# h begins 16 bytes inside a larger tile, 80 bytes in front of the weights modulo 512 in place of 64

## The reference, cut to what matters

```
first block, twice (layer l):
  x += 0.5 * swiglu(rms_norm(x, ffn1_norm), w_gate, w_up, w_down)      # 1024 -> 2816 -> 1024
  h  = rms_norm(x, mix_norm);  a, g, q, k, v = split(h @ w_in)
  x += concat(conv_module(a, g), diff_attention(q, k, v)) @ w_out
  x += 0.5 * swiglu(rms_norm(x, ffn2_norm), ...)
second block, layer 0 and layer 1:
  h  = rmsnorm(x, norm_mix) * (1 + scale) + shift                      # scale, shift, gate from c
  x += gate * (retention_mixer(h) if layer 0 else sgu_mixer(h))
  h  = rmsnorm(x, norm_ffn) * (1 + scale) + shift
  x += gate * peer_ffn(h)          # 16384 experts: queries, top 16 of each of 8 heads, then
                                   # sum over the chosen experts of gelu(h . u_e) * g_e * v_e
x = rmsnorm(x, norm_final)
```

## The kernel before, in words

| tile | address before | modulo 512 |
|---|---|---|
| h_hi, h_lo | 12416, 20608 | 128, 128 |
| w_hi, w_lo | 64192, 80576 | 192, 192 |
| arena | 97408 | 128 |
| p_hi, p_lo (in the arena, float 29456 on) | 215232 on | 192 |

## Time and profile before

### The profile page before, as it was taken

One profiled execution on the slowest core, in us unless ns is written; L12 is line 12 of the kernel. 1 busy time (PEld: TensorE's weight loads), 2 busy tenths in 40 slices (PEclk: granted clock), 3 DMA queues, 4 the chain that ended last, 5 costly groups with the idle time before them and its releaser, 6 DMA issues.

```text
span 3093.0 us, 53282 instructions
## 1 busy us (share of the span) xinstructions
PE 3027.7 (98%) x22540; PEld 2855.6 (92%) x22540; DVE 2184.9 (71%) x3454; ACT 1605.3 (52%) x2383; POOL 274.3 (9%) x255
## 2 busy tenths in 40 slices
PE   8999999999999999999999999999999999999998
PEld 8998999999999898999999998878989998999887
DVE  5877887876887656799555557765659985555676
ACT  5565554565554454456544445547444554444444
POOL 0010001010101001830000000000157000000000
PEclk9999999999999999999999999999999999999999
DMA  6762577774377445457866657545445677666663
GB/s 236 262 245 96 204 268 257 272 268 164 120 258 264 170 142 177 151 178 285 289 217 218 218 204 245 204 176 186 164 156 185 224 295 244 218 216 216 221 232 123
DMA packets 153260, 654.59 MB, mean 212 GB/s; under 512 B 10332, under 2 KB 77472, under 8 KB 78272
## 3 DMA queue, kind: packets, MB, share of 16 engines
q1 hardware_dynamic: 96576, 584.09, 53.1%
q10 hardware_dynamic: 56032, 65.66, 6.3%
q0 software_dynamic: 416, 1.45, 0.1%
HBM read 616.55 MB, written 34.61 MB: 211 GB/s over the span
## 4 chain that ended last, share of the span: by engine, by line
PE 88%; DVE 7%; ACT 2%; POOL 1%; issue 1%; DMA 0%; ACTq 0%; DVEq 0%
PE ps L595 19%; PE ps L597 19%; PE ps L596 19%; PE ps L600 8%; PE ps L601 8%; PE ps L602 8%; PE ps L1022 2%; DVE w_lo L1529 2%; PE ps L761 2%; POOL w_lo L2113 1%; ACT w_hi L1091 1%; DVE h_lo L1547 0%; DVE at L2002 0%; DVE at L2006 0%; PE ps L993 0%
## 5 line engine op out<-in xcount | busy, mean ns | idle before, releaser
L1529 DVE TENSOR_TENSOR w_lo<-raw,w_hi 128x1024 fp32r<-128x1024 f32 x932 | 1137.0, 1227 | 592.4 <-ACT w_hi L1091 591.4
L1091 ACT ACTIVATE w_hi<-raw 128x1024 fp32r<-128x1024 f32 x1000 | 1050.9, 1055 | 699.8 <-PE ps L597 440.9
L595 PE MATMUL ps<-h_hi,w_hi 128*128 128x256 f32 x4224 | 1187.9, 281 | 14.1 <-DVE w_lo L1529 8.6
L596 PE MATMUL ps<-h_lo,w_hi 128*128 128x256 f32 x4224 | 1178.7, 279 | 0.0
L597 PE MATMUL ps<-h_hi,w_lo 128*128 128x256 f32 x4224 | 1178.6, 279 | 0.0
L595 PEld LDWEIGHTS ps<-h_hi,w_hi 128*128 128x128 f32 x4224 | 796.6, 189 | 20.2 <-issue 6.4
L597 PEld LDWEIGHTS ps<-h_hi,w_lo 128*128 128x128 f32 x4224 | 802.7, 190 | 0.0
L596 PEld LDWEIGHTS ps<-h_lo,w_hi 128*128 128x128 f32 x4224 | 795.8, 188 | 2.9 <-issue 0.2
L600 PE MATMUL ps<-w_hi,at 128*128 128x512 f32 x1024 | 398.5, 389 | 3.1 <-DVE at L2059 3.1
L601 PE MATMUL ps<-w_lo,at 128*128 128x512 f32 x1024 | 398.4, 389 | 0.0
L602 PE MATMUL ps<-w_hi,at 128*128 128x512 f32 x1024 | 398.4, 389 | 0.0
(11 more groups left out here) (279 smaller groups left out, 3262.8 us busy)
## 6 DMA issues: line engine op xcount, KB each, us to landing
raw<-in_peer_u SPq DMA_DIRECT2D x128, 1024.0 KB, 4.8
raw<-in_peer_v SPq DMA_DIRECT2D x128, 1024.0 KB, 4.8
raw<-in_ffn_gu SPq DMA_DIRECT2D x88, 1024.0 KB, 4.9
raw<-in_ada_w SPq DMA_DIRECT2D x48, 1024.0 KB, 5.0
raw<-in_ffn_down SPq DMA_DIRECT2D x44, 1024.0 KB, 5.0
gates<-at ACTq DMA_DIRECT2D x32, 1024.0 KB, 4.8
at<-gates ACTq DMA_DIRECT2D x24, 1024.0 KB, 6.0
raw<-in_w_in SPq DMA_DIRECT2D x16, 1024.0 KB, 5.0
```

The lines of the kernel that those rows point to most:

```text
L595: e.matmul(o, lhs[0], rhs[0], start=start, stop=False)
L596: e.matmul(o, lhs[0], rhs[1], start=False, stop=False)
L1091: e.activation(whi[:, u % NPAIR, :], raw(k, half), ACT.Copy).then_inc(hi_done.hit(u), 1)
L1529: e.tensor_tensor(wlo[:, m % NPAIR, :], raw(k, half), whi[:, m % NPAIR, :].bitcast(FP), ALU.subtract).then_inc(w_lo_dve.hit(m), 1)
```

## The change

The two tiles `h_hi` and `h_lo` become the halves of one tile `h_hi_lo` that is 8 floats (32 bytes) longer, and h begins 4 floats (16 bytes) inside it. In front of it a tile `apart` of 120 floats (480 bytes) is taken, which nothing reads or writes.

```diff
         x = sb("x", [128, KT, T])
-        hh_ = sb("h_hi", [128, KT, T], FR)
-        hl_ = sb("h_lo", [128, KT, T], FR)
+        sb("apart", [128, 120])
+        h2 = sb("h_hi_lo", [128, 2 * KT * T + 8], FR)[:, 4:4 + 2 * KT * T].rearrange("p (z k t) -> p z k t", z=2, k=KT)
+        hh_, hl_ = h2[:, 0], h2[:, 1]
         sq = sb("sq", [128, 2, T])
         tmp_h = sb("tmp_h", [128, 3, T])
```

## The result

Four executions of the changed kernel took 3131.07 to 3138.92 us, median 3131.57 us; beside them the kernel before took 3087.3 to 3096.59 us, median 3095.18 us. The ratio is 1.0123, 95% interval 1.0105 to 1.0141: slower, by 1.2%. The forecast was 3130 us. The total came out; two of its terms did not, and their errors nearly cancelled.

The account below looks back on a forecast made before the run. The prediction took TensorE, running matmuls nearly back to back, as the bound. Its terms 29.6 + 4.5 + 1 + 0 gave +35.1 us, from 3094.8 to 3130 us; the range was 3059 to 3141 us.

Parts of the forecast that it names:

- What bounds: Whole kernel: the time is the number of TensorE matmuls times the distance between two starts; TensorE busy 3027.7 of 3093.0 us.
- the likeliest case: Most stretches with h moving fall to 117.8 ns: 3110 to 3135 us, likeliest 3130, chance 0.40.
- Term 1: 12,983 undisturbed matmuls with h moving: between -28.4 and +29.6 us; all at the slower distance was taken, +29.6 us.
- the quick rhythm: 128x256 matmuls starting about 113.3 ns apart; before the change 6,622 of those with h moving.
- the old slow rhythm: 128x256 matmuls starting about 117.8 ns apart; before the change 6,361 of those with h moving.
- a rival with a chance of 0.08: Matmuls with h moving get a third, slower distance of 120 ns: +58 us, 3153 us; chance 0.08, mixtures included.
- Term 2: 3,446 undisturbed matmuls with activations moving take over the rhythm of the stretch before: +4.5 us, between -6.3 and +9.1.
- the bound that the prediction did not take: Matmuls with activations moving: the 1,410 slow ones rise to about 113.3 ns, -6.3 us.
- Term 3: 576 matmuls of 128x512 with h stationary, at 229.6 ns: +1 us, between -1.6 and +2.1.
- Term 4: Writing h, 80 slices by ScalarE and 80 by VectorE at 480 to 500 ns each: 0 us.
- The picture that led to term 1's sign: A guess: stream and stationary load disturb each other where they meet modulo 512; distance 0 is clean, 80 worse than 64.
- The two rules: Skill pages against any effect: 16-byte cachelines give 0; separate TensorE read ports for stream and load give a sum of 0.

Follow-up runs that it names:

- all_back16: Against the kernel before, h, weights and arena all 16 bytes earlier (112, 176, 112 modulo 512), their distances kept; 3079.08 us, ratio 0.9945.
- h_256: Against the kernel before, h alone moved from 128 to 256 modulo 512, 64 bytes behind the weights; 3122.44 us, ratio 1.0084.
- all_fwd16: Against the kernel before, h, weights and arena all 16 bytes further (144, 208, 144 modulo 512), their distances kept; 3078.15 us, ratio 0.9946.
- h_144: Against the kernel before, h alone moved from 128 to 144 modulo 512, 48 bytes in front of the weights; 3130.88 us, ratio 1.0112.
- h_192: Against the kernel before, h alone moved from 128 to 192 modulo 512, distance 0 to the weights; 3141.25 us, ratio 1.0139.
- all_back64: Against the kernel before, h, weights and arena all 64 bytes back (64, 128, 64 modulo 512), their distances kept; 3132.67 us, ratio 1.0122.

## Why the prediction was right, point by point

**What bounds.** Right: TensorE's start distances make the whole difference, 36.4 of 36.3 us, and every other engine only waits longer.

The range of the prediction, 3059 to 3141 us, took in a gain as well as a loss, and "slower" had a chance of 0.48 in it, 0.40 of that for the likeliest case. That the time lay inside says little; the terms say more.

**Term 1, h as the moving side.** The step is right (the change takes the quick rhythm away from h) and its size is not: the sum took +29.6 us, with all h matmuls falling to the old slow rhythm of 117.8 ns. They fell to a third one, 119.2 ns on the mean, which the prediction had as a rival with a chance of 0.08, at 120 ns. The reason it gave for that rival, that h no longer starts on a multiple of 64, isn't the cause: in all_back16 h starts at the same 112 and has 113.56 ns. Undisturbed that is 12,983 x 3.68 = +47.8 us. 6.5 us of it came back, with 38 fewer starts stretched by a wait: TensorE's waits for w_lo went from 8.7 and 5.4 to 4.4 and 4.5 us, as one would expect where a slower TensorE leaves more time to the weights' producers. Net +41.3.

**Term 2, the activations.** Wrong in sign: +4.5 forecast, -4.5 measured. The prediction had a stretch take over the rhythm of the one before it. Quick is followed by quick and the slow rhythm by slow in the earlier trace rows, but the third rhythm hands over to the quick one: 155 to 205 us is at 113.2 ns behind 119.4. The share of quick activations went from 0.59 to 0.87: most of the way to the bound that the prediction did not take, all quick at -6.3 us. Nor is taking over a rule between the two old rhythms: in h_256 the activations behind a quick stretch of h run at 117.9 ns, and behind a slow one at 113.3. What decides it stays open.

**Term 3, h as the stationary side.** +1 us forecast, +0.3 measured (230.0 against 229.7 ns). The prediction read the excess over 226.7 ns as the price of the distance of 64; all_back16 and all_fwd16 have that distance too, and 226.9 ns. So the distance alone is not what costs there.

**Term 4, writing h.** 0 forecast. The line of VectorE in the profile after:

```profile
L1548 DVE SCALAR_TENSOR_TENSOR h_hi_lo<-x,cols,h_hi_lo x48: 471/487/965, 11.3 to 847.6; 128x256 fp32r<-128x256 f32 x48
```

487 ns against 486 in the earlier trace rows, and ScalarE's 495 against 496: right.

So 29.6 + 4.5 + 1 = 35.1 was close to 41.3 - 4.5 + 0.3, with 0.6 and -1.3 from elsewhere, because an underestimate and a wrong sign met. The time alone would have hidden both.

**The reason given.** The picture that led to term 1's sign, that the stream gains on the load and must start at its place or just in front, is refuted by h_144 (slower, where it said faster) and h_192 (slowest of the seven, where it said best). The forecast had the right sign for a wrong reason. What the runs support in its place is narrower: the pair of starts matters, of the distances tried only 64 (in front or behind) opens the quick rhythm to h, and the change leaves it.

**The two rules.** The Trainium skill, "SBUF — State Buffer", "Who interferes with whom", has stream and load on ports of their own that never wait. The runs disagree in effect: all_back16 and the change differ in no instruction and not in h's place, only in where the weights and the arena lie, and the h matmuls run at 113.6 against 119.2 ns. Whether the ports or something behind them is the cause, no run here shows. The 16-byte lines of the same page ("Specifications (TRN2)") would have given 0 for every kernel of the table, since all starts are multiples of 16; they span 76 us from best to worst in profiled time.

**What stays open.** Why 64 and not another distance, why 64 behind is so much less often quick than 64 in front (0.08 against 0.51), whether the weights or the arena is the other side of the pair, and why a start at 16 or 48 past a multiple of 64 gives nearly always the quick rhythm to 64-byte distances and the slower one to p at distance 0 (230 against 226.7 ns). Whether the period is 512 was not tried; h_256 shows only that it isn't 128.

## What to carry to other kernels

Where TensorE runs back to back and loads a new stationary operand for each matmul, measure the distance between starts, not the busy share, and try the addresses of both operands together: here the same instructions took 3065 to 3147 us by place alone. Move the pair, not one side, and look at every kind of matmul, since a place that is good for one distance was bad for another. Read the terms one by one even where the total fits.

## What the runs showed of the hardware that was not expected

- A stream of float32r matmuls with equal instructions, clock and addresses has several steady rhythms: 113.3 and 117.8 ns for 128x256, and for hundreds of matmuls a stretch keeps its own (982 quick ones in a row in before). With h at other distances from the weights the mean was 118.2 to 119.9 ns; for 128x512 it was 226.7 to 233.3 ns, by place.
- A common shift of 16 bytes of all operands, back or forward, took 0.5% off the whole time, with no distance changed.
- In all_back64 two of 32 equal VectorE additions took 23.5 us each, while GpSimd worked without a break, and the other 30 took 988 ns on the mean; the group's mean, 2398 ns, shows neither. In before and the twelve other kernels no such addition took over 1.7 us (group means 968 to 1017 ns).
